# One more step in the gated-attention chain, and a new order of lowerings, banks and loads in a hybrid encoder layer

## The reference

```python
def mixer(xn, ...):
    z = xn @ w_in
    bg, cg, h, q, k, v, gr, r = jnp.split(z, SPLITS, axis=-1)
    cv, conv_new = causal_dwconv(cg * h, conv_prev, conv_w)
    y_conv = rmsnorm(bg * cv, g_conv)
    logg = log_sigmoid(gr @ w_alpha + b_alpha) / GATE_TAU
    o, gla_new = gla(q, k, v, logg, gla_prev)
    y_gla = rmsnorm(o, g_gla) * silu(r)
    return concatenate([y_conv, y_gla]) @ w_out, conv_new, gla_new
# gla, in chunks of 64 rows, with b = cumsum(logg) and b_last its last row:
#   qt = q exp(b);  kt = k exp(-b);  kd = k exp(b_last - b)
#   o  = mask(qt kt^T) v + qt s;     s <- exp(b_last) s + kd^T v
x = x + mixer(rmsnorm(x, norm1), ...)
u = rmsnorm(x, norm2) @ w_up;  uc = causal_dwconv(u, ...);  a, g = split(uc)
x = x + (silu(g) * a) @ w_down;  y = rmsnorm(x, final_norm)
```

## Time and profile before

| | |
|---|---|
| median of 3 runs | 2365.3 us (2362.24 to 2365.51) |
| the profiled execution, its own time | 2365.51 us |
| its span | 2363.8 us |
| mean granted clock of PE | 0.989 |
| busy share of PE, PE weight load, DVE, ACT, POOL | 96%, 88%, 72%, 42%, 51% |
| DMA | 412.73 MB, mean 175 GB/s |
| mixers of blocks 0, 1, 2 | about 0 to 376, 376 to 687, 687 to 899 us |
| FFN | from about 899 us |

### The profile page before, as it was taken

How to read it: one execution, slowest core, us unless ns; L and a number is a source line. 1 busy time by engine, 2 the same in 40 slices (tenths; PEclk the granted TensorE clock), 3 DMA queues, 4 the chain that set the end, 5 groups by cost and what they waited for, 6 DMA issues and landing times. The chain is left out here.

```text
span 2363.8 us, 39571 instructions
## 1 busy us (share of the span) xinstructions
PE 2265.2 (96%) x12602; PEld 2075.6 (88%) x12602; DVE 1700.0 (72%) x2516; ACT 1003.6 (42%) x1957; POOL 1207.2 (51%) x1251
## 2 busy tenths in 40 slices
PE   7998999999999997999999998999999988999997
PEld 6988888988879876899999998999999977999996
DVE  6577765367554665898898988676676777888886
ACT  4544463343534444444444445333333336444443
POOL 2644632214433256777878775444444454555552
PEclk9999999999999998999999999999999999999999
DMA  3643446535367567444444467444444447556553
GB/s 124 198 159 126 168 148 228 178 108 183 133 216 217 162 224 263 155 162 168 160 166 151 160 242 255 153 146 147 157 149 151 147 157 264 183 192 203 184 191 108
DMA packets 264595, 412.73 MB, mean 175 GB/s; under 512 B 14108, under 2 KB 186993, under 8 KB 264497
## 3 DMA queue, kind: packets, MB, share of 16 engines
q1 hardware_dynamic: 264497, 411.45, 51.3%
HBM read 313.24 MB, written 98.16 MB: 174 GB/s over the span
## 5 line engine op out<-in xcount | busy, mean ns | idle before, releaser
L1616 PE MATMUL ps<-xo,wq 128*128 128x384 f32 (+1 forms) x1848 | 601.0, 325 | 27.3 <-POOL wq L999 7.1
L1617 PE MATMUL ps<-xo,wq 128*128 128x384 f32 (+1 forms) x1848 | 599.6, 324 | 0.0
L1618 PE MATMUL ps<-xo,wq 128*128 128x384 f32 (+1 forms) x1848 | 599.2, 324 | 0.0
L2466 DVE TENSOR_TENSOR resid<-resid,ps 128x512 f32<-128x512 f32 (+1 forms) x728 | 477.8, 681 | 73.5 <-PE ps L1618 44.9
L999 POOL TENSOR_TENSOR wq<-wu_raw,wq 128x256 fp32r<-128x256 f32 x396 | 382.6, 988 | 103.6 <-ACT wq L1112 103.6
L1616 PEld LDWEIGHTS ps<-xo,wq 128*128 128x128 f32 x1848 | 351.1, 190 | 49.6 <-POOL wq L999 17.3
L1617 PEld LDWEIGHTS ps<-xo,wq 128*128 128x128 f32 x1848 | 351.8, 190 | 20.2
L1618 PEld LDWEIGHTS ps<-xo,wq 128*128 128x128 f32 x1848 | 351.8, 190 | 0.0
L2483 DVE SCALAR_TENSOR_TENSOR up_y<-up_u,params,up_y 128x768 f32<-128x768 f32 (+1 forms) x264 | 287.5, 1089 | 55.8 <-ACT up_y L1156 37.1
L519 POOL TENSOR_TENSOR wq<-wu_raw,wq 128x256 fp32r<-128x256 f32 x174 | 145.7, 859 | 305.7 <-ACT wq L1233 305.6
L1616 PE MATMUL ps<-wd_hi,hid_hi 128*128 128x512 f32 x704 | 276.3, 393 | 10.5 <-DVE resid L2466 10.5
(11 more groups left out here) (246 smaller groups left out, 4240.3 us busy)
## 6 DMA issues: line engine op xcount, KB each, us to landing
wq<-w_ops SPq DMA_DIRECT2D x176, 512.0 KB, 4.4
wu_raw<-in_w_up_dram SPq DMA_DIRECT2D x89, 512.0 KB, 4.0
w_ops<-wq SPq DMA_DIRECT2D x88, 512.0 KB, 2.6
wq<-m_ops SPq DMA_DIRECT2D x80, 512.0 KB, 3.8
wd_raw<-in_w_down_dram SPq DMA_DIRECT2D x66, 512.0 KB, 5.1
wu_raw<-in_w_in_dram SPq DMA_DIRECT2D x40, 512.0 KB, 4.9
m_ops<-wq SPq DMA_DIRECT2D x40, 512.0 KB, 3.0
x_in<-in_x_prompt_dram SPq DMA_DIRECT2D x32, 512.0 KB, 5.3
```

Of the source, the lines that this page charges most:

```text
L1616: pe.matmul(out, lh, rh, start=(first and n == 0), stop=False, skip_group_check=skip)
L1617: pe.matmul(out, ll, rh, start=False, stop=False, skip_group_check=skip)
L1618: last = pe.matmul(out, lh, rl, start=False, stop=end, skip_group_check=skip)
L2466: last = dve.tensor_tensor(resid[0:m, t, s], resid[0:m, t, s], ps[0:m, bank, :], ALU.add)
```

## The change

It has these parts. (1) A step U stands between X and Y of each full tile that has a successor; `gate_sums(t + 1)` moves from Y into it. `gate_exps` then makes only the copy `b_cum` and `k_exp` from PSUM; the three activations for the queries and `decay` become `query_exps`, read `b_cum` in SBUF, and stand in Y behind the wait for both state updates. On DVE `decays` is split into `key_decays` (in U) and `query_decays` (in Y, behind `next_state(t, 1)`). (2) The banks of the output projection go in the order 0, 1, 2, 3, with the waits that follow from it. (3) `low_heads(1)` moves ahead of units 2 and 3 on POOL. (4) On SP `load_up(0, 1)` moves behind the stores of `x_ops` of the last block. (5) `high_up(0, 0, 6)` and its lowering move into the first FFN step. (6) In block 2 the five `low_x` and the two `sum_up` on DVE move ahead of the additions of the second pass.

```diff
@@ -125,11 +125,6 @@
-def out_bank(b, p, n):
-    return (0, 3, 1, 2)[(p * 2 * TILES[b] + n) % 4]
...
@@ -557,7 +552,9 @@
             products = [(p, i) for p in range(NPAIR) for i in range(NP)]
-            steps = [(s, t) for t in range(TILES[b]) for s in ("XYZ" if tile_cols(b, t)[1] == P else "XZ")]
+            steps = [(s, t) for t in range(TILES[b]) for s in ("XUYZ" if tile_cols(b, t)[1] == P else "XZ")
+                     if s != "U" or t + 1 < TILES[b]]
@@ -830,8 +827,6 @@
                         load_x_op(0, i)
-                    sp.wait_ge(wu_lo, splits(0, 0, 5))
-                    load_up(0, 1)
@@ -842,6 +837,8 @@
                 else:
+                    sp.wait_ge(wu_lo, splits(0, 0, 5))
+                    load_up(0, 1)
@@ -974,9 +971,9 @@
                 low_heads(0)
+                low_heads(1)
...
                 low_unit(pool, out_unit(b, 3))
-                low_heads(1)
@@ -1029,7 +1026,7 @@
-            for i in range(NP):
+            for i in range(NP - 1):
@@ -1039,8 +1036,7 @@
                 prev = before(b, f, 1)
-                if prev or b:
-                    low_up(b, f, NP - 1)
+                low_up(b, f, NP - 1)
@@ -1286,15 +1282,21 @@
+                    mix.wait(act, "q_exped", t)
                     mix.wait(act, "dist", t)
+                    mix.wait(act, "att_done", t)
...
-                    act.activation(q_exp[0:HK, :, 0, 0:m], b_ps[0:HK, :, 0:m], ACT.Exp, scale=1 / TAU)
-                    act.activation(q_exp[HK:P, :, 1, 0:m], b_ps[HK:P, :, 0:m], ACT.Exp, scale=1 / TAU)
+                    mix.inc(act.activation(k_exp[:, :, 0:m], b_ps[:, :, 0:m], ACT.Exp, scale=-1 / TAU), "cum_read")
+                def query_exps(t):
+                    m = tile_cols(b, t)[1]
+                    mix.wait(act, "cum_read", t + 1)
...
                     mix.wait(act, "state1", min(t, BTS[b] // P))
-                    act.activation(decay[:, :, 0:m // CHUNK], b_ps[:, :, CHUNK - 1:m:CHUNK], ACT.Exp, scale=1 / TAU)
-                    mix.inc(act.activation(k_exp[:, :, 0:m], b_ps[:, :, 0:m], ACT.Exp, scale=-1 / TAU), "cum_read")
+                    act.activation(q_exp[0:HK, :, 0, 0:m], b_cum[0:HK, :, 0:m], ACT.Exp, scale=1 / TAU)
+                    act.activation(decay[:, :, 0:m // CHUNK], b_cum[:, :, CHUNK - 1:m:CHUNK], ACT.Exp, scale=1 / TAU)
+                    mix.inc(act.activation(q_exp[HK:P, :, 1, 0:m], b_cum[HK:P, :, 0:m], ACT.Exp, scale=1 / TAU), "q_exped")
@@ -1394,6 +1396,7 @@
                         gate_exps(0)
+                        query_exps(0)
@@ -1403,11 +1406,14 @@
                             o_square(t)
+                    if ev[0] == "U":
+                        gate_exps(t + 1)
                     if ev[0] == "Y":
+                        if more:
+                            k_end_exp(t + 1)
                         o_square(t)
-                    if ev[0] == ("Y" if tile_cols(b, t)[1] == P else "X") and more:
-                        gate_exps(t + 1)
-                        k_end_exp(t + 1)
+                        if more:
+                            query_exps(t + 1)
@@ -1503,7 +1509,6 @@
                     high_up(0, 0, 5)
-                    high_up(0, 0, 6)
@@ -1525,8 +1530,7 @@
                     keep_first_product(b, g, par)
-                if not first_of_all:
-                    high_up(b, f, 6)
+                high_up(b, f, 6)
@@ -1659,7 +1663,7 @@
                         elif b:
-                            mixes[b - 1].wait(pe, "out_read", 4 * TILES[b - 1] - (3, 1, 0)[n])
+                            mixes[b - 1].wait(pe, "out_read", 4 * TILES[b - 1] - 3 + n)
@@ -1745,6 +1749,7 @@
                     m = tile_cols(b, t)[1]
+                    mix.wait(pe, "cum_read", t + 1)
@@ -1815,10 +1820,10 @@
                             gate_product(t + 1)
+                    if ev[0] == "U":
+                        gate_sums(t + 1)
...
                         outputs_2(t)
-                        if more:
-                            gate_sums(t + 1)
@@ -1830,8 +1835,8 @@
                     if slots[0] == 0:
-                        if number < 4:
-                            mix.wait(pe, ("c11_read", "turned_read", "c21_read", "c12_read")[number], (NPAIR, nt, NPAIR, NPAIR)[number])
+                        if number < 3:
+                            mix.wait(pe, ("c11_read", "c21_read", "c12_read")[number], NPAIR)
@@ -1841,7 +1846,7 @@
                         k = (SLOTS * p + slot + HEADS) % KT
-                        last = product(ps[0:m, out_bank(b, p, n), :], [
+                        last = product(ps[0:m, number % 4, :], [
@@ -1937,7 +1942,7 @@
                     if edge == 0 and b == 0 and i < 3:
-                        mixes[NB - 1].wait(pe, "out_read", 4 * TILES[NB - 1] - (3, 1, 0)[i])
+                        mixes[NB - 1].wait(pe, "out_read", 4 * TILES[NB - 1] - (3, 2, 0)[i])
@@ -2166,22 +2171,28 @@
-                def decays(t):
+                def key_decays(t):
...
                     mix.wait(dve, "cum_read", t + 1)
+                    mix.wait(dve, "turned", t)
...
                     mix.inc(last, "dist")
+                    dve.tensor_tensor(k_exp[:, :, 0:m], k_exp[:, :, 0:m], qk[:, 2:4, c0:c0 + m], ALU.mult)
+                def query_decays(t):
+                    c0, m = tile_cols(b, t)
+                    mix.wait(dve, "k_end_exp", t + 1)
+                    dve.tensor_tensor(k_end[:, :, 0:m], k_end[:, :, 0:m], qk[:, 2:4, c0:c0 + m], ALU.mult)
+                    mix.wait(dve, "q_exped", t + 1)
...
                         r = slice(e * HK, (e + 1) * HK)
-                        dve.scalar_tensor_tensor(q_exp[r, :, e, 0:m], q_exp[r, :, e, 0:m], HK ** -0.5, qk[r, 0:2, c0:c0 + m],
-                                                 ALU.mult, ALU.mult)
-                    dve.tensor_tensor(k_exp[:, :, 0:m], k_exp[:, :, 0:m], qk[:, 2:4, c0:c0 + m], ALU.mult)
-                    mix.wait(dve, "k_end_exp", t + 1)
-                    mix.inc(dve.tensor_tensor(k_end[:, :, 0:m], k_end[:, :, 0:m], qk[:, 2:4, c0:c0 + m], ALU.mult), "qk_exp")
+                        last = dve.scalar_tensor_tensor(q_exp[r, :, e, 0:m], q_exp[r, :, e, 0:m], HK ** -0.5, qk[r, 0:2, c0:c0 + m],
+                                                        ALU.mult, ALU.mult)
+                    mix.inc(last, "qk_exp")
...
@@ -2335,10 +2347,12 @@
                             log_gate(t + 1)
+                    if ev[0] == "U":
+                        key_decays(t + 1)
...
                         if more:
-                            decays(t + 1)
+                            query_decays(t + 1)
@@ -2364,7 +2378,7 @@
                         prev = resid[0:m, t, cols] if p else x_in[0:m, t % NX, cols]
-                        mix.inc(dve.tensor_tensor(resid[0:m, t, cols], ps[0:m, out_bank(b, p, n), :], prev, ALU.add), "out_read")
+                        mix.inc(dve.tensor_tensor(resid[0:m, t, cols], ps[0:m, (p * 2 * nt + n) % 4, :], prev, ALU.add), "out_read")
@@ -2417,16 +2431,20 @@
+                if not nxt:
+                    for i in range(3):
+                        low_x(0, i)
+                    unit_free(dve, (2, 3), unit_index(NB, "v", 2, 0))
+                    sum_up(0, 0)
+                    sum_up(0, 1)
+                    low_x(0, 3)
+                    low_x(0, 4)
...
                 second_scale(0)
-                if not nxt:
-                    low_x(0, 0)
-                    low_x(0, 1)
@@ -2435,12 +2453,6 @@
                 second_scale(1 + mid)
-                if not nxt:
-                    unit_free(dve, (2, 3), unit_index(NB, "v", 2, 0))
-                    sum_up(0, 0)
-                    sum_up(0, 1)
-                    for i in range(2, 5):
-                        low_x(0, i)
...
                 next_scale(3 + mid)
```

More of the change, by code:

```diff
@@ L406, in mix_counts @@
                 "u_done": 2, "y_first": CJ, "conv_step": 2 * CJ, "y_done": 2, "pre": nt, "pre_b": nt,
-                "soft": 3 * nt, "lg": nt, "cum": nt, "cum_read": nt, "dist": nt, "k_end_exp": nt, "qk_exp": nt,
+                "soft": 3 * nt, "lg": nt, "cum": nt, "cum_read": nt, "dist": nt, "k_end_exp": nt, "q_exped": nt, "qk_exp": nt,
                 "att_done": nt, "att_read": nt, "turned": nt, "turned_read": nt, "d1": nt, "d2": full,
@@ L2318, in pair_event @@
                         mix.wait(dve, "c12_read", 4)
-                        decays(0)
+                        key_decays(0)
+                        query_decays(0)
                 for ev in mix_events(b):
```

## The result

The changed kernel takes 2396.84 us (median of 4 runs, 2394.77 to 2398.27) beside 2365.41 us of the kernel before (4 runs) on the same chip: a ratio of 1.0135, interval [1.0117, 1.0152]. It is slower by 31.4 us. The profiled execution took 2399.06 us itself, 2.2 more than the median; its span is 2397.3 us, 33.5 more than before, and it is these 33.5 that the traces divide up.

What follows compares the result with a forecast made beforehand. The prediction took TensorE, busy 96% of the span, as the bound, so only its idle time and slow clock could change. Its terms, 14 + 6 - 2 = +18 on 2365.5 us, gave 2383 us, range 2362 to 2396.

Steps and rivals of the forecast that it cites:

- Attention chain: Gated attention with step U: fewer products per gap, longer waits for sums, scores and gla_y; +14 us, bounds 0 to 20.
- the clock: Attention chain, slow clock behind waits: block 0 loses 1.2 us against 3.1 before; block 1 falls once in both kernels.
- The activations read from SBUF: Three activations behind b_cum read SBUF, not PSUM: 0.1 us a tile, 1 us in all, left in the rounding.
- Lowering order and banks: Output projection: slot 3 starts 2.3 us later in blocks 0 and 1, 1.6 in block 2, banks hidden; +6 us.
- `low_x` and `sum_up`: Start of the FFN: 14 us moved into VectorE's idle time, later add_out, resid wait about 4 us; net 0 to +1.
- the 2.2, 0.7 and 2.2 us that were to be given back: FFN start: savings from the resid wait (2.2), x_n (0.7) and the first two up products' slow clock (2.2).
- `load_up(0, 1)`: FFN start: the late load fills a DMA hole, so stores of wq come 2 to 3 us earlier; -2.5 us.
- `high_up(0, 0, 6)`: First FFN step: moving it costs nothing, as its lowering ends near 915 and its product starts near 918.
- the late load is the bound: Rival: load_up(0, 1) lands at 924, products wait for weights, FFN starts 5 us later; 2390 us, chance 0.08.
- the chain gets its slack: Rival, faster: the attention chain's three gaps are covered, scores and lg waits and clock falls go; 2351 us, chance 0.15.
- only the lowering order counts: Rival, slightly slower: the chain comes out even, the order costs 6 less 2; 2369 us, chance 0.17.
- gains and losses cancel: Rival: the change as a whole changes nothing; 2365 us, chance 0.10.

Runs made afterwards that it cites:

- undo_f: The whole change without part 6 (the low_x and sum_up move on DVE), timed against the kernel before: 2390.61 us, ratio 1.0106.
- u_step: The kernel before with part 1 only, step U and the split of the decays: 2384.13 us, ratio 1.0077.
- banks: The kernel before with part 2 only, output projection banks in order 0, 1, 2, 3 and their waits: 2366.36 us, ratio 1.0003.
- late_load: The kernel before with part 4 only, load_up(0, 1) behind the stores of the last block: 2366.44 us, ratio 1.0003.
- split_only: The kernel before with activations and decays split, all of U's work in Y behind outputs_2, products dealt as before: 2366.39 us, ratio 1.0005.
- dve_first: The kernel before with part 6 only, five low_x and two sum_up ahead of block 2's second pass: 2372.73 us, ratio 1.0027.
- u_no_share: The kernel before with step U directly ahead of Y but given no products, dealt over X, Y, Z as before: 2373.72 us, ratio 1.003.
- taps_only: The kernel before, no step U, with a bg pair's second convolution taps moved from product 3's event to product 4's: 2368.56 us, ratio 1.0005.
- dve_two: The kernel before with only low_x(0, 0) and low_x(0, 1) ahead of block 2's second pass, no sum_up: 2369.66 us, ratio 1.001.
- order_banks: The kernel before with parts 2 and 3 together, bank order and the low_heads(1) move: 2373.18 us, ratio 1.0026.
- undo_u: The whole change without step U, attention chain as before, timed against the kernel before: 2377.61 us, ratio 1.0034.
- late_high: The kernel before with part 5 only, high_up(0, 0, 6) and its lowering in the first FFN step: 2367.43 us, ratio 0.9995.
- order: The kernel before with part 3 only, low_heads(1) ahead of units 2 and 3 on GpSimd: 2376.21 us, ratio 1.0038.

## Why the prediction was off

The direction and the main mechanism were right, the size was not: +18 forecast, +31.4 measured, above the range's end of 2396 by 0.84 us. By its own terms:

- **Attention chain, +14.** Measured +17.8 alone, and 18.7 in the windows of the kernel after. The mechanism holds: four waits for `lg` of 0.83 to 0.92 us in block 1 (forecast 1.05), all waits for `lg` together +8.6 (forecast 4.0 in block 0, 3.4 in block 1, 1.45 in block 2), and the scores of tile 2 waiting 3.23 and 3.74 (forecast 3.9), put down to "issue" and not to `q_exp`. The waits for `gla_y` did not grow by the forecast 0.95 and 1.75 in blocks 0 and 1 but by 0.1 in all; so waits, forecast at 6.3 + 6.6 + 2.7 = 15.6 more, are 11.4 more. The term of this sum that was off is the clock: block 0 was to gain 1.9 us of it and blocks 1 and 2 to stay even, and by the granted clock about 3, 0 and 2 us were lost, some 7 above the forecast. By the same count `undo_f` lost about 3.5 us there and `u_step` about 1, so the size is not settled, but none of the three gained clock. The falls behind tile 2's scores are not the new ones, for the kernel before has them at the same two places (the earlier trace rows and the window at 502.10 further down). In this profile the new ones stand behind a wait of 3.51 us for `lg` in tile 0 of block 0 and behind one of 2.16 us for `gla_y` in block 2:

```profile
145.60:151.60 6.00, 5.96 (x23) 5.96 (x24) 3.19 (x6) 2.85 (x8) 5.84 (x8) 0.54 0.52 170
802.40:808.40 6.00, 5.93 (x31) 5.40 (x32) 3.49 (x8) 0.00 (x0) 0.00 (x0) 0.72 0.15 57
```

  The first of them is in part chance. The forecast for that wait was 2.0 us, and in `u_step` it is 1.86 with the clock at 1.00 behind it. In the kernel after, VectorE stood still before it for a load:

```profile
139.39 0.69 DVE L2126 TENSOR_TENSOR wu_sum<-wu_raw 128x512 f32<-128x512 f32 x1 [1.82 <-DMA wu_raw<-in_w_in_dram]
```

  This wait is 0.17 us in the kernel before and in `u_step`, but 1.72 in `banks` and 1.62 in `late_load`, which change nothing in that part, so it comes without step U too. By block, the stretches forecast at 4.4, 6.6 and 3 us more came out at 7.2, 5.6 and 5.9 in the kernel after, 2.9, 5.6 and 7.7 in `u_step`, and 6.2, 5.6 and 5.8 in `undo_f`: block 1 was forecast 1 us too high and block 2 3 to 5 us too low in each of them, of which waits are 0.7 (3.4 for 2.7) in the kernel after.

- **The activations read from SBUF, 0.1 us a tile, left in the rounding.** `split_only` has them and measures -0.4 us in all: no cost that can be seen.
- **Lowering order and banks, +6 (2.3, 2.3, 1.6).** Measured +10.4 for the order alone and +6.9 with the banks, with intervals that overlap, and 3.7, 2.2 and 2.0 by the trace. The mechanism and two of the three sizes are right; the first lacked 1.5 us of clock behind a wait of 2.76, and where the clock falls in block 2 as well, as in the changed kernel, the third lacks it too: 3.7, 2.2 and 3.3 there. The banks' 0.7 a block is hidden, and by less cover than forecast.
- **`low_x` and `sum_up`, net 0 to +1.** Measured +6.4. This is the step that failed. The prediction counted VectorE's 14 us and placed them in its idle time, and it saw that `low_x` runs "beside a busy GpSimd"; it took from there a longer time for VectorE alone, and put what GpSimd loses, and TensorE's wait for it, at nothing without a reason. GpSimd was busy with the weights that TensorE needs next, and they came 4.5 us late. The wait for `resid` of about 4 us is there (3.64), but 3.2 us of waits for `w_lo` come before it. Of the 2.2, 0.7 and 2.2 us that were to be given back, `dve_first` has the first, for no product waits at the start of its FFN, but its waits for `x_n` grew from 18.2 to 19.4 us in all. By its trace the start of the FFN gives back 2.1 of the 6.9.
- **`load_up(0, 1)`, -2.5; `high_up(0, 0, 6)`, 0.** Both measure 0 within 2 to 3 us. For the load, the idle DMA between 918 and 921 was read as room whose filling brings the stores behind it forward; the stores of `wq` were issued at the same time with the load moved. The rival that the late load is the bound was right in its mechanism and wrong in its price: the first product of step 1 waits 3.67 us for the load, and the wait that follows in any case hides it.

The 13.4 us between forecast and result are 5.9 from the VectorE move (6.4 for 0.5), 3.8 from the chain (17.8 for 14, clock above and waits below), 2.5 from the load's gain that did not come, and 0.9 from the lowering order (6.9 for 6), 13.1 by this count. The chain and the lowering order had the right mechanism and a size within a third; the VectorE move had the wait for `w_lo` missing, and the load's gain rested on stores that did not move.

The rivals: that the chain gets its slack is out (`split_only` measures -0.4 and `u_no_share` +7.4); that only the lowering order counts is out by the chain's 17.8; that the late load costs 5 us is out by `late_load` (+0.6, with an interval up to 3), and that gains and losses cancel by the result.

## What to carry to other kernels

Work that is dealt out evenly between dependent steps is cover, and a new step takes its share from every other gap: count the products in each gap before and after, since here the dealing alone cost 12.6 us. Ask also what stands behind a new wait: the sums ahead of `outputs_2` cost 7.4 us with the old dealing. Before filling idle time on VectorE, look at which lists of GpSimd run at that moment and who waits for them; here each of VectorE's subtractions, 2.6 us long, cost GpSimd 1.5. A wait of 2 to 4 us on TensorE is to be priced with the clock behind it, but as a chance and not as a certainty.

## What the runs showed of the hardware

- GpSimd and VectorE subtracting side by side: GpSimd's eight of 128x512 take 14.52 us for 10.03, VectorE's of 128x1536 2.63 us each for 1.71, nearly one engine at a time. The profile shows it only as longer instructions, not as waits.
- The clock does not fall behind every wait of one length. Behind a wait of 2.70 us for the scores in block 1 of the kernel before the six microseconds ran at 0.77, and in `taps_only`, behind a wait of 2.72 us at the same place, at full clock, which is 1.4 us between two kernels whose matmuls are the same there. Ten profiles have this wait with 2.70 to 2.72 us: the clock fell behind it in five (the kernel before, `dve_first`, `dve_two`, `order_banks`, `undo_u`) and not in five (`banks`, `late_high`, `late_load`, `order`, `taps_only`). The two windows, the kernel before:

```profile
502.10:508.10 6.00, 6.00 (x31) 6.00 (x31) 4.83 (x10) 1.39 (x3) 1.88 (x2) 0.77 0.18 32
```

  and `taps_only`:

```profile
501.50:507.50 6.00, 6.00 (x42) 6.00 (x41) 5.74 (x10) 1.39 (x3) 2.56 (x2) 1.00 0.26 90
```

  By such falls the attention stretch of block 1 is between 1.6 us shorter (`banks`, `late_high`, `late_load`, `order`, `taps_only`) and 1.2 longer (`dve_two`) than in the kernel before, over profiles of kernels with the same work there, so a stretch of one profiled execution is not read closer than that. The start of the FFN varies more: up to about the sixtieth matmul of its `w_down` products it took between 3.6 us less (the kernel after) and 1.4 more (`dve_two`) than in the kernel before.
